# Score products issued after the value products in each attention step

## The reference

```
s = einsum('btkgd,bskd->bkgts', q, k) * HEAD_DIM ** -0.5 + bias     # score products
s = where(mask, s, -inf)                                            # band (A) or selected keys (B)
p = exp(s - max(s)); p = p / sum(p)                                 # A adds exp(sink - m) to the sum
out = einsum('bkgts,bskd->btkgd', p, v)                             # value products
mixed = concatenate([oa * silu(ga), ob * silu(gb)])                 # gating
y = LayerNorm(ALPHA * x + gate * (mixed @ w_out))
```

## Time and profile before

| | before |
|---|---|
| median of three runs | 2010.36 us (2007.12 to 2012.75) |
| the profiled execution | 2015.11 us |
| its span in the trace | 2013.4 us |
| PE, DVE, ACT, POOL busy over the span | 94%, 48%, 31%, 34% |
| attention, group A | about 1231 to 1335 us of the span |
| attention, group B | about 1335 to 1583 us of the span |

### The profile page before, as it was taken

The page is one execution under the profiler, slowest core; times in us unless marked ns, Lnnn a source line. Parts: engine busy times, 40 slices in busy tenths (PEclk is TensorE's granted clock), DMA queues, the critical chain, the costliest instruction groups (busy, mean ns, idle before and its releaser), DMA issues.

```text
span 2013.4 us, 35908 instructions
## 1 busy us (share of the span) xinstructions
PE 1883.3 (94%) x13143; PEld 1568.7 (78%) x13143; DVE 971.5 (48%) x2488; ACT 625.1 (31%) x1349; POOL 676.6 (34%) x850
## 2 busy tenths in 40 slices
PE   4999999999999999999999998989999899999992
PEld 0666787759999999999999996656665688888772
DVE  0333403467777788885000003987776233342826
ACT  0121233331111111111111115988887422222220
POOL 0122211112222222222222224866666544444741
PEclk7888899979999999999999999999999999999996
DMA  8666233103232222232222244431211244446463
GB/s 268 200 214 211 74 112 111 38 17 93 86 91 85 85 85 85 85 90 85 85 85 87 89 128 95 112 94 47 57 41 30 79 121 120 120 126 175 125 216 90
DMA packets 198320, 213.22 MB, mean 106 GB/s; under 512 B 22128, under 2 KB 145520, under 8 KB 197376
## 3 DMA queue, kind: packets, MB, share of 16 engines
q1 hardware_dynamic: 177648, 177.16, 31.6%
q10 hardware_dynamic: 19232, 30.30, 4.0%
q0 software_dynamic: 1328, 4.26, 0.7%
HBM read 181.31 MB, written 34.55 MB: 107 GB/s over the span
## 4 chain that ended last, share of the span: by engine, by line
issue 45%; PE 26%; POOL 17%; ACT 5%; DVE 4%; DMA 2%; POOLq 1%; SPq 0%; ACTq 0%; DVEq 0%
POOL w_lo L1003 8%; POOL w_lo L1052 8%; PE psum L1562 4%; PE psum L1519 3%; PE psum L1541 3%; PE psum L1400 2%; PE psum L1402 2%; PE psum L1401 2%; PE psum L1428 2%; DMA ada_ring<-in_w_ada_dram 2%; PE psum L1360 2%; ACT p_rows L898 1%; PE psum L1430 1%; PE psum L1429 1%; PE psum L1383 1%
## 5 line engine op out<-in xcount | busy, mean ns | idle before, releaser
L1428 PE MATMUL psum<-h_hi,w_hi 128*128 128x364 f32 (+1 forms) x1728 | 578.0, 334 | 7.6 <-POOL w_lo L1003 7.0
L1430 PE MATMUL psum<-h_lo,w_hi 128*128 128x364 f32 (+1 forms) x1728 | 567.8, 329 | 0.0
L1429 PE MATMUL psum<-h_hi,w_lo 128*128 128x364 f32 (+1 forms) x1728 | 566.3, 328 | 0.0
L1003 POOL TENSOR_TENSOR w_lo<-w_raw,w_hi 128x512 fp32r<-128x512 f32 x144 | 185.5, 1289 | 708.3 <-ACT w_hi L757 708.0
L1428 PEld LDWEIGHTS psum<-h_hi,w_hi 128*128 128x128 f32 x1728 | 326.0, 189 | 45.4 <-issue 36.8
L1429 PEld LDWEIGHTS psum<-h_hi,w_lo 128*128 128x128 f32 x1728 | 326.1, 189 | 0.0
L1430 PEld LDWEIGHTS psum<-h_lo,w_hi 128*128 128x128 f32 x1728 | 325.8, 189 | 0.0
L1052 POOL TENSOR_TENSOR w_lo<-w_raw,w_hi 128x512 fp32r<-128x512 f32 x128 | 180.3, 1409 | 208.6 <-ACT w_hi L943 208.6
L757 ACT ACTIVATE w_hi<-w_raw 128x512 fp32r<-128x512 f32 x144 | 90.7, 630 | 480.9 <-PE psum L1430 454.1
L1147 DVE MAX8 top<-scores 128x8 f32<-128x384 f32 (+6 forms) x210 | 185.4, 883 | 83.5 <-DVE scores L1150 83.3
L1611 PE MATMUL psum<-w_hi,mixed_halves 128*128 128x512 f32 x512 | 201.7, 394 | 10.7 <-POOL w_lo L1052 10.7
(11 more groups left out here) (205 smaller groups left out, 2676.7 us busy)
## 6 DMA issues: line engine op xcount, KB each, us to landing
w_raw<-in_w_in_dram SPq DMA_DIRECT2D x160, 256.0 KB, 2.9
ada_ring<-in_w_ada_dram SPq DMA_DIRECT2D x64, 512.0 KB, 5.0
w_raw<-in_w_out_dram SPq DMA_DIRECT2D x256, 128.0 KB, 2.9
z_transposed<-z_evacuated ACTq DMA_DIRECT2D x32, 544.0 KB, 2.7
stage<-in_w_ada_dram SPq DMA_DIRECT2D x32, 512.0 KB, 4.0
over_z_evacuated<-z_transposed SPq DMA_DIRECT2D x32, 272.0 KB, 4.4
x_block<-in_x_prompt_dram SPq DMA_DIRECT2D x4, 2048.0 KB, 8.5
q_transposed<-z_transposed SPq DMA_DIRECT2D x16, 272.0 KB, 4.6
```

What stands on the lines that cost most here:

```text
L1003: pool.tensor_tensor(v(wlo), raw3[ch][:, :, 0:width], v(whi).bitcast(F32), ALU.subtract).then_inc(lo_ready.sem, 1)
L1428: pe.matmul(Z, w(whi), hh[:, kt_, a:b], start=(kt_ == 0), stop=False)
L1429: pe.matmul(Z, w(wlo), hh[:, kt_, a:b], start=False, stop=False)
L1430: ins = pe.matmul(Z, w(whi), hl[:, kt_, a:b], start=False, stop=(kt_ == KT - 1))
```

## The change

In a turn of a step TensorE does the transposes, then the value products that are due, and the score products last. Nothing else changes: the same instructions, the same waits in front of each, and the lists of the other engines are the same.

```diff
@@ -1571,8 +1571,6 @@
             for j in range(max(len(due), nc_)):
                 if j < len(due):
                     transposes(due[j])
-                if j < nc_:
-                    q_k(step, j)
                 if step < NA and not due:
 
                     last = max([b for b, ks in enumerate(BATCHES) if T_STEP[PIECES[ks[0]][0]] < step], default=0)
@@ -1583,6 +1581,8 @@
                     for b in range(done, due[j]):
                         p_v(b)
                     done = due[j]
+                if j < nc_:
+                    q_k(step, j)
         p_v(done)
 
         pe.wait_ge(min_ready.sem, min_ready.at(2 * CHUNK_AT[NI]))
```

## The result

The changed kernel took 2046.27 us (median of 4, 2041.01 to 2050.47) against 2011.55 for the kernel before on the same chip: 1.0168 times as long, interval 1.0149 to 1.0188, or 34.7 us more. The forecast was 17.3 more. The profiled execution took 2046.04 us with a span of 2044.4, 31.0 more than before; both projections kept their lengths, and the attention began 2.0 us earlier.

What follows compares the result with a forecast made beforehand. It took three nearly full engines to bound group A and TensorE group B, its order deciding who waits. A's 7.9 us plus B's 9.4 made 17.3, on 2010.36 about 2028 us; range 2011 to 2042.

Steps and rivals of the forecast that it cites:

- The ring: Group A: gate, value products, even score products, scoring, reciprocal, next gate, 3.18 us a round (3.13 mean); chance 0.70.
- the pairs with tables: Group A, pairs where VectorE also prepares bias tables: 3.07 us of work anyway, costed at nothing, 0.11 at most.
- 0.33 us a pair: Group A, pairs without tables: 3.13 us against 2.80 before; over 24 pairs 7.9 us.
- The rival that ScalarE holds A: Group A: ScalarE sets the time, so only B's 9.4 us count, 2020 us; chance 0.12.
- the rule of the highest occupancy: Skill's rule: the busiest engine is the bottleneck; ScalarE would set A's time, leaving B's 9.4 us alone.
- The second turns: Group B, second turns at S4, the next step and S5: late gates cost 0.58, 0.39 and 0.21, 1.18 us a head pair.
- S5, where I had 0.21: Group B, second turn of S5: value products wait for a late gating until 1452.19, 0.21 us more lost.
- all of S7 is 0.21 late. TensorE loses nothing: Group B, step S7: VectorE starts at 1428.66 instead of 1428.45, at no cost to TensorE.
- S6, S3, S2 and S8 keep their distance: Group B, these steps: no further loss after 0.97 us; values gated a step earlier, or gate lags as much as TensorE.
- S4's wait: Group B, S4's second turn: TensorE stands until the gate allows tile 8's value products at 1432.44; 0.58 us lost.
- I take them as the others: Group B, last two head pairs: three instead of two such turns, yet counted at 1.18 us each like the rest.
- The rival in which the hole is filled: Both groups: value products use the score products' waits, half of 12.9 us recovered, 2004 us; chance 0.07.

Runs made afterwards that it cites:

- e1: Kernel before, with the new order only in the steps that score group A: 1.0056 times the kernel before, 2023.35 us.
- e5: Kernel before, with the new order only in group B's second to sixth head pair: 1.0045 times the kernel before.
- e9: Kernel before, with the new order only in second turns of group B's steps (second chunks of tiles 4 to 8): 1.0048 times the kernel before.
- e6: Kernel before, with the new order only in group B's first and last two head pairs: 1.0070 times the kernel before.
- e8: Changed kernel, with three batches of transposes issued 3, 6 and 3 times over where TensorE waits between groups A and B: 1.0154 times the kernel before.
- e11: Kernel before, with three long TensorE waits filled with transposes that do nothing: 0.9973 times the kernel before, 2006.34 us.
- e10: As e8, plus three batches of transposes issued 2, 7 and 4 times over in B's seventh head pair: 1.0157 times the kernel before.
- e3: Changed kernel, with VectorE's gate one step earlier (old gate kept for A's last eight items): 1.0014 times the kernel before.
- e4: Kernel before (old order), with the same earlier gate as e3: 1.0101 times the kernel before.
- e2: Kernel before, with the new order only in the steps that score group B: 1.0127 times the kernel before, 2037.95 us.

## Why the prediction was wrong

The direction and the mechanism were right, the size was half: 17.3 us forecast, 34.7 measured, above the upper end of the range. By its terms, in the profiled executions:

- **A, 7.9 forecast, 10.2 measured (e1: 9.8).** The ring is there, step by step, and the pairs with tables cost nothing, as I had them. The term that failed is a size, 0.33 us a pair: the other seven of nine went from 2.77 to 3.23, 0.46 each. A full round takes 3.26 instead of 3.18, and 2.80 was too high for the old round, because I took 3.07 for both pairs with tables. The rival that ScalarE holds A is out: its share fell from 14.58 to 13.56 of 15 us while A grew, so the sum by the rule of the highest occupancy, B's term alone, does not hold here.
- **B, the five steady head pairs: 5.9 forecast, 8.7 measured (e5: 9.5 by its time).** The second turns came out near the sum, 1.12 in e9 against 1.18, though no wait for the gate shows at S5, where I had 0.21. The step that failed is "all of S7 is 0.21 late. TensorE loses nothing" and with it the sentence that S6, S3, S2 and S8 keep their distance. I followed one head pair from an undisturbed start and didn't close the round: the lateness of S5's second chunk meets the next head pair's first step (the wait at 1442.75), and S4's wait, worked out as 0.96 (1432.44 against 1431.48), became 1.22.
- **B, the first and the last two head pairs: 3.5 forecast, 14 measured (e6: 16.2).** This is the largest miss. Of the last two I wrote "I take them as the others", and the first was counted with the rest without a word. At the change from A to B the ring runs through two-chunk scorings, and TensorE's waits grew by 2.1 us; with the clock (2.5) and the moved border (1.0) that makes the 5.6. In the seventh head pair its waits grew from 3.2 to 5.9 us, and with the clock (2.2) that makes 4.9 of the 5.0. In the eighth they grew from 2.7 to 5.0, at full clock up to the last microsecond (1.00 over 1571.7 to 1604.3), so its 3.3 us are waits in the main. The last two orders have fewer steps between scoring and transposes, which would fit longer waits; no run tests that.
- **The clock, not forecast at all.** Of the 14 us, about 2.5 (e8 and e11) and 2.2 (e10) were TensorE at the lower clock behind such waits. The profile of before already had 0.77 and 0.89 in two windows of the attention; I left these rows unread, priced a longer wait at its length alone, and so had no term for what follows it.

The signs named ahead came as said: ScalarE's share near 90%, VectorE's waits for L1519 about once a pair, waits for the gate of some tens of us in the whole attention, S4's chunk (1418.94) 0.61 behind the value products that had waited for the gate (1418.33). Two head pairs of A at 27.9 was too low. The rival in which the hole is filled had a core: with the gate moved as well (e3), A and B's middle are shorter than before.

Open: whether the last two head pairs lose by their shorter way from scoring to transposes; what e3 would take with the earlier gate at the change from A to B as well; where the part of e11's gain arises that its profile doesn't show; and what more than two slots in PSUM for the value products would do, which wasn't tried.

## What to carry to other kernels

When two operations change places on one engine, look for a third engine's operation that waits for the one and releases the other: the order on TensorE and the gate's step on VectorE are one choice, and either alone was worse (e4 and the changed kernel) than both or none. Close a replay around at least two rounds, and replay the seams by themselves; a steady round says nothing on a place where large and small items meet. Where the granted clock falls behind waits in the profile of before, a change that lengthens waits on TensorE can pay for them twice (e8, e10), and work that does nothing may be cheaper than standing still (e11).

## What the runs showed of the hardware

The same waits of TensorE (0.86, 2.12 and about 1.6 us in the seventh head pair) were followed by the lower clock in the changed kernel's profile (0.62 over 1549 to 1558) and not in e10's (1.00 over 1546 to 1553). Over the whole seventh head pair the mean granted clock was 0.91 in the profiles of the changed kernel, e2 and e6, 0.95 in e8's and 1.00 in e10's, with the same order there. So the waits alone don't decide whether the clock falls. e3, with long waits in the first head pair, varied most, 2009.74 to 2025.84 us in ten runs; that the clock is the reason is not shown, as its fastest and its slowest run both have a mean of 0.967 over the whole execution. With three waits filled with transposes that nobody reads (e11) the clock was at 1.00 in all three windows, and the time was 0.27% shorter.
